# Norms fed from inside the matmul pairs, four modulation blocks moved to TensorE, matmuls without use in the gaps, and a result stored in four parts

## The chip, the cores and the metric

The kernel runs on one core of one Trainium2 chip. The metric is the device time of one execution in microseconds (us). Three executions of the kernel before are shown, and one more that was profiled.

## What is computed

Two layers of a decoder trunk at width 1024, 256 positions, batch 1, all in float32. What matters here is the frame around the mixers:

```python
for l in range(DEPTH):                       # 2 layers
    mod = (c_act @ w_mod[l] + b_mod[l])[:, None, :]       # 1024 x 6144 matrix times one vector
    sh1, sc1, gt1, sh2, sc2, gt2 = jnp.split(mod, 6, axis=-1)
    h = rmsnorm(x, norm1_g[l]) * (1 + sc1) + sh1
    z = h @ w_cat                            # then three mixers: RG-LRU, attention, RWKV-7
    ...
    x = x + gt1 * (merged @ w_out[l])
    h2 = rmsnorm(x, norm2_g[l]) * (1 + sc2) + sh2
    x = x + gt2 * conv_gated_mlp(h2, ffn_up[l], ffn_conv_w[l], ffn_conv_b[l], ffn_down[l])
return rmsnorm(x, final_g)
```

So there are five norms: before and after the mixers of each layer, and one at the end. Each needs a sum of squares over all 1024 channels, and nothing behind it can start before that sum.

## The kernel before

The residual stream X and the normed input H lie in SBUF as 8 tiles of 128 channels by 256 positions. The weights come in "pairs" of 1 MB, 75 for each layer, through a ring of four slots that the SyncE queue (SP) fills; the slot of pair g may be refilled when pair g - 4 is done. A pair makes two output tiles (m = 0 and 1) in one PSUM bank, g % 4. Pairs 35 to 38 of a layer (`OU`) are the output projection, 39 to 62 (`UP`) the up projection, 63 to 74 (`DN`) the down projection. In these three each factor is split into a high and a low part: ScalarE copies the high half (`out_high`, `high`, lines L642 and L666), VectorE subtracts the low one (`out_low`, `low`, L1157 and L1196), and TensorE runs three passes (`passes`, L1305 to L1307) of 8 matmuls for each tile, 48 for a pair. The other pairs are plain float32 matmuls (L1318, L1428); the profile shows two records for each of those.

Every engine has its own instruction list, written out in a fixed order, with counting semaphores between them. Around the change the order is this:

- ScalarE in the output projection: `out_high(0)`, `out_high(1)`, the high parts of the merged input, `out_high(2)`, `out_high(3)`, `high(0, 0, True)`, `high(0, 1, True)` (the first two pairs of the up projection), and only then `squares(2 * l + 1)`. `out_high(3)` waits for the second pair of the projection to be done, since it overwrites its weights; `high(0, 1, True)` waits for its ring slot, which is refilled after that same pair.
- ScalarE in the down projection: `high` of the last pair, whose second half waits for the end of the pair two before it, then `squares` of the next norm.
- VectorE: `residual(g, j, scale)` adds the two tiles of pair j to X (L1184), between the `low` calls; then `norm` makes H (L840) and, for the second norm of a layer, the low part `HL` (L1209).
- TensorE: after the last pair of a projection `ones_sum(n)` sums the 8 squared tiles with a matrix of ones (L1289), 8 matmuls that each wait for their square.

`squares(n)` squares X tile by tile, waits for the sum, takes Ln (L451), then Exp with scale -0.5 (L453) for the inverse root. `shifts` adds the modulation vector (L464, L465).

The modulation vectors are made beside all that. Each of the 12 vectors (`unit` u) is a sum over 8 blocks of 128 x 1024: VectorE multiplies a block with a scalar per partition and adds it to `macc` (L803 for the first block of a unit, L806 for the others), and `mod_sum` on TensorE (L1283) sums `macc` over the partitions with 8 matmuls of one column. Units 0 and 1 are needed for the first norm; their 16 blocks come in 8 transfers of 1 MB at the beginning. The others come through `mring`, two slots filled from GpSimd's queue, and `mod_beside(n)` puts n blocks between other work of VectorE. 16 of these blocks lie in the down projection of layer 0 (`DN_BLOCKS`), and the last `mod_sum(7)` comes after its last pair.

## Time and profile before

| what | us |
| --- | --- |
| median of three executions | 1295.5 |
| lowest and highest of them | 1282.28 and 1296.42 |
| the profiled execution, its whole time | 1285.15 |
| its span from the first to the last instruction | 1283.3 |
| TensorE busy in the span | 1197.8 (93%) |
| VectorE busy | 716.7 (56%) |
| ScalarE busy | 451.7 (35%) |

The span is what the trace covers; 1.85 us of the profiled execution lie around it. In the trace PE is a matmul on TensorE, PEld a weight load, DVE VectorE, ACT ScalarE, POOL GpSimd, and a q behind a name its queue. "PEclk" is the granted clock of TensorE as a share of 2.4 GHz: 1.00 is 2.4 GHz and 0.50 is 1.2 GHz.

### The profile page before, as it was taken

How to read it: one execution, taken by the hardware profiler on the slowest of the kernel's cores; microseconds unless marked ns; L12 is line 12 of the kernel's file. 1: busy time of each engine (PE TensorE's matmuls, PEld its weight loads, DVE VectorE, ACT ScalarE, POOL GpSimd, SP SyncE). 2: the span in 40 equal slices, each digit the busy share in tenths (PEclk: the TensorE clock that was granted, in tenths of full speed). 3: DMA queues.
4: the chain of work that ended last, by engine and by line, in shares of the span. 5: the costliest groups of instructions: out<-in, count | busy, mean ns of one | idle time of the engine just before them, and what ended most of it. 6: DMA issues, size and time to landing. Idle time of an engine off the chain costs nothing.

```text
span 1283.3 us, 23717 instructions
## 1 busy us (share of the span) xinstructions
PE 1197.8 (93%) x9976; PEld 1088.6 (85%) x9976; DVE 716.7 (56%) x1112; ACT 451.7 (35%) x747; POOL 65.8 (5%) x108
## 2 busy tenths in 40 slices
PE   2899999998999799999989999999899979999996
PEld 2788888877788799999968788888787879999996
DVE  5565545365236578777536482625522556778643
ACT  2222234401113666654232221450012156666532
POOL 0000000011010000001100000000100200000000
PEclk8799999999999899999989999999889999999998
DMA  9655444154135355557835454234512453454530
GB/s 381 258 206 187 165 141 178 45 208 154 66 127 183 152 195 177 182 187 290 294 113 188 174 188 166 106 132 155 169 56 84 147 215 121 175 196 166 194 132 33
DMA packets 38897, 214.57 MB, mean 167 GB/s; under 512 B 6144, under 2 KB 6400, under 8 KB 19232
## 3 DMA queue, kind: packets, MB, share of 16 engines
q1 hardware_dynamic: 27296, 171.42, 36.9%
q0 software_dynamic: 11520, 41.95, 9.5%
q8 instruction: 65, 1.06, 0.3%
q14 instruction: 16, 0.13, 0.0%
HBM read 212.30 MB, written 1.05 MB: 166 GB/s over the span
## 4 chain that ended last, share of the span: by engine, by line
PE 86%; DMA 5%; DVE 5%; issue 1%; ACT 1%; SPq 0%; DVEq 0%; ACTq 0%
PE ps L1318 19%; PE ps L1428 12%; PE ps L1305 12%; PE ps L1306 11%; PE ps L1307 11%; PE ps L1629 6%; DMA mring<-wmod_dram 4%; DVE macc L806 3%; PE ps L1514 3%; PE ps L1283 2%; PE ps L1289 1%; DMA G<-wmod_dram 1%; DVE H L840 1%; PE ps L1505 1%; PE ps L1439 1%
## 5 line engine op out<-in xcount | busy, mean ns | idle before, releaser
L1318 PE MATMUL ps<-H,ring 128*128 128x256 f32 x1088 | 244.4, 386 | 5.0 <-ACT H L465 5.0
L1318 PEld LDWEIGHTS ps<-H,ring 128*128 128x128 f32 x1088 | 210.0, 194 | 41.4 <-issue 12.6
L1196 DVE TENSOR_TENSOR WLO<-ring,WH 128x1024 fp32r<-128x1024 f32 x144 | 175.1, 1222 | 101.2 <-ACT WH L666 101.0
L1305 PE MATMUL ps<-HH,WH 128*128 128x256 f32 x768 | 219.5, 286 | 12.5 <-DVE HL L1209 12.5
L1306 PE MATMUL ps<-HL,WH 128*128 128x256 f32 x768 | 219.2, 285 | 0.0
L1307 PE MATMUL ps<-HH,WLO 128*128 128x256 f32 x768 | 219.1, 285 | 0.0
L666 ACT ACTIVATE WH<-ring 128x1024 fp32r<-128x1024 f32 x144 | 151.8, 1058 | 170.8 <-PE ps L1307 168.7
L1428 PE MATMUL ps<-H,ring 128*128 128x256 f32 x768 | 182.6, 390 | 0.0
L1428 PEld LDWEIGHTS ps<-H,ring 128*128 128x128 f32 x768 | 144.1, 193 | 22.7 <-issue 1.8
L1305 PEld LDWEIGHTS ps<-HH,WH 128*128 128x128 f32 x768 | 149.4, 195 | 13.3 <-issue 13.3
L1306 PEld LDWEIGHTS ps<-HL,WH 128*128 128x128 f32 x768 | 149.4, 195 | 0.0
L1307 PEld LDWEIGHTS ps<-HH,WLO 128*128 128x128 f32 x768 | 149.3, 194 | 0.0
L806 DVE SCALAR_TENSOR_TENSOR macc<-mring,sm,macc 128x1024 f32<-128x1024 f32 x70 | 89.8, 1283 | 46.2 <-DMA mring<-wmod_dram 43.2
L1305 PE MATMUL ps<-GH,WH 128*128 128x256 f32 (+1 forms) x384 | 108.7, 283 | 0.0
L1306 PE MATMUL ps<-GL,WH 128*128 128x256 f32 (+1 forms) x384 | 108.7, 283 | 0.0
L1307 PE MATMUL ps<-GH,WLO 128*128 128x256 f32 (+1 forms) x384 | 108.7, 283 | 0.0
L400 POOL DMA_DIRECT2D mring<-wmod_dram x80 | 42.5, 532 | 796.3 <-DVE macc L803 403.4
L563 ACT ACTIVATE G<-ps 128x512 f32<-128x512 f32 x24 | 14.1, 594 | 190.3 <-PE ps L1428 190.1
L1224 DVE SCALAR_TENSOR_TENSOR TK<-ps,PR,TK 128x255 f32<-128x255 f32 x192 | 79.1, 474 | 0.1
L1514 PEld LDWEIGHTS ps<-R 64*64 64x64 f32 x1792 | 57.2, 140 | 20.9 <-DVE R L1082 14.9
L1306 PEld LDWEIGHTS ps<-GL,WH 128*128 128x128 f32 x384 | 73.7, 192 | 0.0
L1307 PEld LDWEIGHTS ps<-GH,WLO 128*128 128x128 f32 x384 | 73.7, 192 | 0.0
(297 smaller groups left out, 1537.2 us busy)
## 6 DMA issues: line engine op xcount, KB each, us to landing
ring<-wmain_dram SPq DMA_DIRECT2D x150, 1024.0 KB, 4.8
mring<-wmod_dram POOLq DMA_DIRECT2D x80, 512.0 KB, 4.9
G<-wmod_dram SPq DMA_DIRECT2D x3, 1024.0 KB, 9.7
R<-wmod_dram SPq DMA_DIRECT2D x3, 1024.0 KB, 18.1
TK<-wmod_dram SPq DMA_DIRECT2D x2, 1024.0 KB, 23.1
C<-consts_dram SPq DMA_DIRECT2D x1, 1088.5 KB, 18.2
X<-x_t_dram SPq DMA_DIRECT2D x1, 1024.0 KB, 12.0
SW<-small_dram SPq DMA_DIRECT2D x2, 512.0 KB, 15.0
```

What stands on the lines that cost most here:

```text
L400: pool.dma_start(mring[:, n % 2, :], wmod[n]).then_inc(s_m[n % 2], 16)
L666: A(WH[:, n % 2, part], ring[:, b, part], ACT.Copy).then_inc(hi_ready, 1)
L806: V.scalar_tensor_tensor(macc[:, :], block, sm[:, CSIL + kt:CSIL + kt + 1], macc[:, :], ALU.mult, ALU.add).then_inc(mod_used, 1)
L1196: V.tensor_tensor(WLO[:, n % 2, part], ring[:, b, part], WH[:, n % 2, part].bitcast(F32), ALU.subtract).then_inc(lo_ready, 1)
L1224: ins = V.scalar_tensor_tensor(UB[:, q % 2, t, d:S], duo(b)[:, t, 0:S - d], PR[:, l, bass.ds(j + (COL["fw"] + 48 * (2 - d)), 1)], UB[:, q ...
L1305: MM(out, w_high[:, at], high, start=start, stop=False, skip_group_check=True)
L1306: MM(out, w_high[:, at], low, start=False, stop=False, skip_group_check=True)
L1307: return MM(out, w_low[:, at], high, start=False, stop=stop, skip_group_check=True)
L1318: last = MM(ps[:, g % 4, m * S:(m + 1) * S], w_of(g, m, i), rhs[:, i, :], start=(i == 0), stop=(i == KT - 1))
L1428: last = MM(ps[:, g % 4, m * S:(m + 1) * S], w_of(g, m, i), H[:, i, :], start=(i == 0), stop=(i == KT - 1))
L1514: last = MM(ps[halves[c], b, m * 64:(m + 1) * 64], a[halves[c], m, :], bb[halves[c], m, :], start=True, stop=True)
L1629: last = MM(ps[:, b, (m % 2) * S:(m % 2 + 1) * S], w_of(g, m, k, 4), y[:, k, :], start=(k == 0), stop=(k == 3))
```

## The change

1. **Beginning.** `macc` has two buffers, one for even and one for odd units. Four of the first 16 blocks (3, 7, 11, 15, `DIRECT`) no longer go through VectorE; `mod_direct` multiplies them on TensorE straight into the bank of their unit, 8 matmuls of one column each. GpSimd waits for the last of the first transfers before it loads `mring`. The first weight pair is issued ahead of the constants. The first four tiles of H may be made before unit 1 is known. 18 matmuls without use (`keep_clock`) lie between the parts.
2. **Norms.** `squares` and `ones_sum` no longer wait for the whole projection. After pair 1 of the last four TensorE sums tiles 0 and 1, after pair 2 tiles 2 and 3, between the two halves of pair 3 tiles 4 and 5, then 6 and 7. Tile 7 gets a bank of its own (`residual_ps`), so that tile 6 can be read while tile 7 is summed. ScalarE loads the table of Ln ahead of the squares, and `Acol` is made ahead of the residuals.
3. **Second norm of a layer.** HL is made by VectorE from the unshifted H, so ScalarE writes only HH. The first up pair (`up_first`) does its passes with HH first and those with HL after them.
4. **Gaps.** `keep_clock(8)` after three of the sums of squares in the two layers.
5. **Modulation in layer 0.** 10 of the 16 blocks move from the down projection into the up projection (`UP_BLOCKS`), whose VectorE loop is unrolled; the other 6 go one to each of the first six down pairs. `mod_sum(6)` comes after down pair 1 and `mod_sum(7)` after down pair 6.
6. **Output.** Four transfers of 256 KB, each when its two tiles are ready, in place of one of 1 MB.

```diff
+DIRECT = (3, 7, 11, 15)
+UP_BLOCKS = [0] * 4 + [1, 0] * 10
+DN_BLOCKS = [1, 1, 1, 1, 1, 1, 0, 0, 0, 0, 0, 0]
+DN_SUM, DN_LAST = 1, 6
+LOGARITHM = "natural_log"
...
+        def residual_ps(g, j, i):
+
+            return ps[:, 5, 0:S] if (j, i) == (3, 1) else ps[:, g % 4, i * S:(i + 1) * S]
...
+            sp.dma_start(ring[:, 0, :], wmain[0]).then_inc(s_w[0], 16)
             sp.dma_start(C[:, :], consts).then_inc(s_par, 16)
...
-            sp.wait_ge(h_pre, 8 * 5)
-            sp.dma_start(y_t, H[:, :, :]).then_inc(s_out, 16)
-            sp.wait_ge(s_out, 16)
+            for j in range(4):
+                sp.wait_ge(h_pre, 8 * 4 + 2 * j + 2)
+                sp.dma_start(y_t[:, 2 * j:2 * j + 2, :], H[:, 2 * j:2 * j + 2, :]).then_inc(s_out, 16)
+            sp.wait_ge(s_out, 64)
...
+            pool.wait_ge(s_first[7], 16)
...
             def squares(n):
 
+                if n:
+                    act.preload_act_table_set(LOGARITHM)
+                else:
+                    act.wait_ge(s_x, 16)
                 for m in range(KT):
-                    if n:
+                    if n and m % 2 == 0:
+                        act.wait_ge(x_tile, 4 * (n - 1) + m // 2 + 1)
+                    elif n:
                         g = PAIRS * ((n - 1) // 2) + (OU if n % 2 else PAIRS - 4) + m // 2
                         act.wait_ge(bank_free[g % 4], EMPTIED[g][g % 4] + 1)
-                    if m == 0 and n:
-                        act.wait_ge(pair_done, PAIRS * ((n - 1) // 2) + (OU + 4 if n % 2 else PAIRS))
-                    elif m == 0:
-                        act.wait_ge(s_x, 16)
                     A(H[:, m, :], X[:, m, :], ACT.Square).then_inc(x_sq, 1)
...
-                    V.tensor_tensor(HL[:, m, :], H[:, m, :], HH[:, m, :].bitcast(F32), ALU.subtract).then_inc(hl_ready, 1)
+                    V.scalar_tensor_tensor(HL[:, m, :], H[:, m, :], mod[:, u, m:m + 1], HH[:, m, :].bitcast(F32),
+                                           ALU.add, ALU.subtract).then_inc(hl_ready, 1)
...
+            def mod_direct(n):
+
+                u, kt = divmod(n, 8)
+                pe.wait_ge(s_first[n // 2], 16)
+                for j in range(KT):
+                    MM(ps[:, 7 - u, j:j + 1], first_blocks(n // 2)[:, n % 2, j * P:(j + 1) * P], sm[:, CSIL + kt:CSIL + kt + 1],
+                       start=(n % 8 == DIRECT[0] and j == 0), stop=False, skip_group_check=True)
...
+            def keep_clock(n, b, moving):
+
+                for _ in range(n):
+                    MM(ps[:, b, 0:S], ones[:, :], moving, start=True, stop=True, skip_group_check=True)
...
+                    pe.wait_ge(c_ready, 1)
+                    mod_direct(3)
+                    ones_sum(0)
+                    keep_clock(6, 5, X[:, 0, :])
+                    mod_direct(7)
+                    keep_clock(2, 5, X[:, 0, :])
                     mod_sum(0)
+                    keep_clock(4, 5, X[:, 0, :])
+                    mod_direct(11)
+                    keep_clock(6, 5, X[:, 0, :])
+                    mod_direct(15)
                     mod_sum(1)
...
+                        if (j, m) == (3, 0):
+                            last.then_inc(out_half, 1)
+                            ones_sum(2 * l + 1, 4, 6)
                     last.then_inc(pair_done, 1)
-                ones_sum(2 * l + 1)
+                    if j:
+                        ones_sum(2 * l + 1, (0, 2, 6)[j - 1], (2, 4, 8)[j - 1])
+                keep_clock(8, 6, C[:, 0:S])
...
+                for q in range(4):
+                    down(2, q, tail=True)
+                    if q:
+                        ones_sum(2 * l + 2, (0, 2, 6)[q - 1], (2, 4, 8)[q - 1])
+                if l == 0:
+                    keep_clock(8, 6, C[:, 0:S])
```

## Rows read from the trace of the kernel before

**Rows 1.** The page: busy time and share of two engines.

```profile
PE 1197.8 (93%) x9976; PEld 1088.6 (85%) x9976; DVE 716.7 (56%) x1112; ACT 451.7 (35%) x747; POOL 65.8 (5%) x108
```

**Rows 2.** Timeline of the beginning: start, duration, engine, line, what, idle before.

```profile
6.71 0.75 DVE L803 TENSOR_SCALAR macc<-G,sm 128x1024 f32<-128x1024 f32 x1 [2.19 <-DMA G<-wmod_dram]
...
11.43 2.67 DVE L806 SCALAR_TENSOR_TENSOR macc<-G,sm,macc 128x1024 f32<-128x1024 f32 x2 [2.57 <-DMA G<-wmod_dram]
...
30.51 5.45 DVE L806 SCALAR_TENSOR_TENSOR macc<-TK,sm,macc 128x1024 f32<-128x1024 f32 x4
...
36.01 3.57 PE L1283 MATMUL ps<-sm,macc 128*128 128x1 f32 x16 [10.65 <-DVE macc L806]
...
41.07 30.70 PE L1318 MATMUL ps<-H,ring 128*128 128x256 f32 x128 [1.48 <-ACT H L465]
```

**Rows 3.** The last first-block transfers (tile TK): issue range, and time to landing.

```profile
L342 SPq DMA_DIRECT2D TK<-wmod_dram x2: 482/4467/8452, 5.0 to 5.5; - x2
...
DMA to landing us min/median/max: 22.1/23.1/24.1
```

**Rows 4.** The chain of work: start, duration, what; plain matmuls and `mod_sum` at 2.4 GHz.

```profile
97.30 1.68 PE ps L1283 x16
...
132.05 13.81 PE ps L1318 x64
```

**Rows 5.** ScalarE's timeline around the second norm of layer 0.

```profile
408.79 1.92 ACT L642 ACTIVATE OWH<-ring 128x2048 fp32r<-128x2048 f32 x1 [3.84 <-PE ps L1307]
410.61 1.99 ACT L666 ACTIVATE WH<-ring 128x1024 fp32r<-128x1024 f32 x2
413.66 2.01 ACT L666 ACTIVATE WH<-ring 128x1024 fp32r<-128x1024 f32 x2 [1.06 <-DMA ring<-wmain_dram]
420.58 2.56 ACT L449 ACTIVATE H<-X 128x256 f32<-128x256 f32 x8 [4.92 <-PE ps L1307]
...
425.30 1.28 ACT L453 ACT_TABLE_LOAD   x1
426.60 0.42 ACT L453 ACTIVATE RT<-RT 128x256 f32<-128x256 f32 x1
...
439.11 1.06 ACT L666 ACTIVATE WH<-ring 128x1024 fp32r<-128x1024 f32 x1 [1.75 <-PE ps L1307]
```

**Rows 6.** VectorE's timeline around the same norm.

```profile
407.25 0.87 DVE L1184 SCALAR_TENSOR_TENSOR X<-ps,sm,X 128x256 f32<-128x256 f32 x2
...
427.11 3.26 DVE L840 SCALAR_TENSOR_TENSOR H<-X,Acol,RT 128x256 f32<-128x256 f32 x8 [5.92 <-ACT RT L453]
```

**Rows 7.** The chain of work there: split passes before and after, and the sum of squares.

```profile
419.97 0.12 PE ps L1306
...
421.05 3.73 PE ps L1289 x16
...
430.85 0.55 PE ps L1305
```

**Rows 8.** Windows: us, busy PE, PEld, DVE, ACT, POOL, granted clock, DMA share, GB/s.

```profile
26.00:36.00 10.00, 0.00 (x0) 0.00 (x0) 9.23 (x8) 0.00 (x0) 0.00 (x0) 0.50 1.03 416
...
428.00:430.00 2.00, 0.00 (x0) 0.00 (x0) 2.00 (x6) 2.00 (x6) 0.00 (x0) 0.77 0.61 258
```

**Rows 9.** Between the layers: ScalarE's last weight half; then the chain of work.

```profile
630.95 1.06 ACT L666 ACTIVATE WH<-ring 128x1024 fp32r<-128x1024 f32 x1 [1.76 <-PE ps L1307]
...
655.79 4.60 PE ps L1318 x10
```

**Rows 10.** VectorE in the up projection of layer 0: its only idle time in a tile.

```profile
457.48 1.23 DVE L1196 TENSOR_TENSOR WLO<-ring,WH 128x1024 fp32r<-128x1024 f32 x1 [1.17 <-ACT WH L666]
```

**Rows 11.** The end: when ScalarE takes the last weights, last norm, store.

```profile
1257.78 1.06 ACT L666 ACTIVATE WH<-ring 128x1024 fp32r<-128x1024 f32 x1 [1.76 <-PE ps L1307]
...
1275.82 3.25 DVE L840 SCALAR_TENSOR_TENSOR H<-X,PR,RT 128x256 f32<-128x256 f32 x8 [5.64 <-ACT RT L453]
...
y_dram<-H SPq DMA_DIRECT2D x1, 1024.0 KB, 3.9
```

More of the change, by code:

```diff
@@ L100, with added @@
 EMPTIED = _emptied()
+def added(n):
+    return n + 1 - sum(d <= n for d in DIRECT)
 FILL = [4, 16, 24, 16, 16, 4, 12, 8] + [8] + [3, 5, 4] * 4 + [6, 6, 0]
@@ L1248, in _ @@
                     up_tile(0, q, True)
-                with dve.Fori(1, FT // 4) as i:
-                    for q in range(4):
-                        up_tile(i, q)
+                if l == 0:
+                    for n in range(4, FT):
+                        up_tile(n // 4, n % 4)
+                        mod_beside(UP_BLOCKS[n])
+                else:
+                    with dve.Fori(1, FT // 4) as i:
+                        for q in range(4):
+                            up_tile(i, q)
                 hidden_low(0, FT - 2)
@@ L1672, in up @@
                         for k in range(KT):
-                            if first and q == 0 and m == 0:
-                                pe.wait_ge(hl_ready, KT * l + k + 1)
                             last = passes(ps[:, b, m * S:(m + 1) * S], WH[:, q % 2, :], WLO[:, q % 2, :], m * KT + k, HH[:, k, :], HL[:, k, :], k == 0, k == KT - 1)
                         last.then_inc((half_done, pair_done)[m], 1)
-                for q in range(4):
-                    up(0, q, True)
+                up_first()
+                for q in range(1, 4):
+                    up(0, q)
                 with pe.Fori(1, FT // 4) as i:
@@ L1682, in _, with down @@
                         up(i, q)
-                def down(i, q, first=False):
+                def down(i, q, first=False, tail=False):
                     g = PAIRS * l + DN + q
@@ L1695, in down @@
                             at = k if first else bass.ds(i * 8 + k, 1)
[L1696 to L1697 removed]
+                            last = passes(residual_ps(g, q, m), WH[:, q % 2, :], WLO[:, q % 2, :], m * KT + k, GH[:, at, :], GL[:, at, :],
+                                          first and k == 0 and (m == 0 or q == 3), False)
                         last.then_inc((half_done, pair_done)[m], 1)
+                        if (tail, q, m) == (True, 3, 0):
+                            ones_sum(2 * l + 2, 4, 6)
                 for q in range(4):
                     down(0, q, True)
+                    if l == 0 and q == DN_SUM:
+                        mod_sum(6)
+                pe.wait_ge(g_ready, FT * (l + 1))
                 if l == 0:
[L1703 to L1712 removed]
+                    for q in range(4):
+                        down(1, q)
+                        if 4 + q == DN_LAST:
+                            mod_sum(7)
+                else:
+                    with pe.Fori(1, 2) as i:
                         for q in range(4):
                             down(i, q)
[L1715 removed]
+                for q in range(4):
+                    down(2, q, tail=True)
+                    if q:
+                        ones_sum(2 * l + 2, (0, 2, 6)[q - 1], (2, 4, 8)[q - 1])
+                if l == 0:
+                    keep_clock(8, 6, C[:, 0:S])
 def kernel(x, c, positions, w_mod, b_mod, norm1_g, norm2_g, final_g, w_in, w_merge_a, w_merge_b, w_merge_c, w_out,
```

135 lines of the change are left out of this document (74 added, 61 removed).

## The prediction

> **What bounds the kernel now.** I read the page first. TensorE is busy for 93% of the span and VectorE for 56% [rows 1], so time can come only from places where TensorE waits or runs slowly. The timeline then shows where those are. The one long wait is at the beginning: TensorE's product starts at 41.07 us, behind a modulation sum at 36.01 that waited 10.65 us for VectorE's blocks [rows 2]. The others are the four later norms. At the one in layer 0 the split passes end at 420.1 and the next begins at 430.85; between them lie 3.73 us of sums of squares [rows 7] and ScalarE's chain of Ln, a table load and Exp [rows 5]. The windows show a second cost of each gap: the granted clock is 0.50 (1.2 GHz) while TensorE is nearly idle at the beginning, and falls within 428 to 430, in the gap behind the sum of squares [rows 7, 8]. Then work restarts slowly: the first 10 records of layer 1 take 4.60 us [rows 9], 0.46 each, against 13.81 / 64 = 0.216 at the full 2.4 GHz [rows 4].
>
> Unit prices at full clock: a plain matmul is two records, 0.432 us; a split pass 0.12 [rows 7], so a pair of 48 is 5.76; a `mod_sum` 1.68 [rows 4], and a `mod_direct` issues the same 8 one-column matmuls, so I take 1.68 for it too.
>
> **Beginning (part 1).** The last two first-block transfers are issued at 5.0 and 5.5 and land 22.1 and 24.1 us later [rows 3], at 27.1 and 29.6. Block group 1 landed 4.72 us after group 0 (6.71 and 11.43, [rows 2]), where 2.56 separate others (27.1 to 29.6): the 1 MB of `mring` went in between. Holding it back moves the last group to about 27.05. VectorE then has 12 blocks for 16, at 5.45 / 4 = 1.36 each [rows 2], and is no longer last: block 14 ends at about 28.5. What is last is either the landing or TensorE's own list. By the landing: 27.05 + 1.68 + 1.68, then the vector, ScalarE's shift and the start, together 41.07 - 39.6 = 1.5 less what is made ahead (0.8), gives a start at 31.3. By the list: it opens with group 1 (8.9) and holds 4 directs and 2 sums (10.1 us), 8 matmuls of squares (3.5) and 18 without use (7.8), 21.4 us at full clock, and some 4.5 us of it run at half speed first (2.3 lost): the sum ends at 32.6, and the start is 33.4. The list is later and I take it: 41.07 - 33.4 = 7.7. If the clock is also kept, the four first pairs take 27.6 (128 x 0.216) in place of 30.70 [rows 2], 3.1 more. Together **-10.8**. The bounds: 9.8 + 3.1 = -12.9 by the landing alone, and nearly nothing (-2) if the useless matmuls don't bring the clock up, since each of the list's parts then takes double. The added wait of GpSimd holds only `mring` loads that nobody needs for 15 us; the weight pair now ahead of the constants delays `derived`, which has the first pair's 7 us as cover.
>
> **Second norm of a layer (parts 2 to 4).** This is where I expect a wait in the place of the one removed. TensorE now stops after pair 1 of the output projection for squares 0 and 1. ScalarE reaches its squares only behind `out_high(3)`, `high(0, 0)` and `high(0, 1)`, and the first of these itself starts when that pair ends: 408.79, then 410.61, then 413.66 (after a transfer that is issued at the same moment), done at 415.67 [rows 5]. Behind it comes the table load that the change puts ahead of the squares, 1.28 [rows 5], and one square, 2.56 / 8 = 0.32 pitch and 0.42 long: TensorE goes on at about 417.5, idle for **8.7 us**. VectorE is not to blame, its first residual ends at 408.1 [rows 6]. Before, the same engine time of ScalarE lay beside pairs 2 and 3. In the shorter gap from 424.8 to 430.85 the granted clock fell from 1.00 to 0.50 [rows 7, 8], so this one costs the clock as well: 2.3 (half of 4.6, [rows 9]).
>
> From there: second square and sum to 418.4; pair 2 with the clock loss 5.76 + 2.3, to 426.4; sums of tiles 2 and 3, 0.86; half of pair 3, 2.88; sums of 4 and 5, 0.86; second half to 433.9. Behind it only tile 7: residual 0.48 [rows 6], square 0.42, one sum 0.43 and the handovers, 1.4, to 435.3. Ln, load and Exp take what they take now (424.78 to 427.02, 2.24 [rows 5, 7]), to 437.55. H, HH and the start: 1.2, to 438.75. `up_first` follows ScalarE's pace of 0.4 for 8 tiles, 3.1, then 16 + 16 + 8 and some passes, in all 6.85: the first up pair ends at 445.6. Before it ended at 439.05 (ScalarE's wait for it ends at 439.11 [rows 5]). So this norm **loses 6.6** in each layer, although its tail behind the last pass shrinks (420.1 to 430.85 was 10.7; 433.9 to 438.75 is 4.9). Both: **+13.2**, with layer 1 taken as equal. `keep_clock(8)` is 3.46, inside the 3.45 from 435.3 to the start, so it costs nothing and keeps the up projection at full clock.
>
> The load ahead of the squares sits in this stall, but without it it would sit behind them. The row prices it at 1.28 and lets the next activation begin 1.30 after its start (425.30, 426.60 [rows 5]). The Trainium skill, ScalarE: Activation LUTs, section "What ACT_TABLE_LOAD costs", gives about 2.66 for every switch to a different set, with a drain behind the load. The trace does not agree (1.30); by the page each stall would be 1.4 longer, +5.5 in the four norms.
>
> **Between the layers (parts 2, 4, 5).** ScalarE's last weight half starts when the second of the last four pairs has ended, 630.87 [rows 9]; `mod_sum(7)` now lies ahead of that, so 632.55. From this point, called E: weight half and table load to E + 2.4; VectorE's low half and first residual to E + 2.8; squares; TensorE idle until E + 3.3, sums to E + 4.2. Then 5.76 + 0.86 + 2.88 + 0.86 + 2.88 to E + 17.4; tile 7 and its sum to E + 18.85; Ln, load, Exp to E + 21.1; H, shift and start 1.25: E + 22.35 = 654.9. Before, the product started at 655.79 [rows 9]: 0.9 won. With the clock kept another 2.9, as at the beginning (4.60 - 10 x 0.216 = 2.4, and a little behind it). **-3.8**. What is removed here is VectorE's late last block and the sum of all eight squares behind the last pass; what comes is the 3.3 stall.
>
> **Up projection (part 5).** Ten blocks of 1.28 or less join VectorE, one in two tiles. A tile has 1.17 idle there [rows 10], two have 2.3, so the block fits; the low weight halves are wanted some 5 us later than they are made. Zero. If that cover is gone, 10 x 1.28 = 12.8. `mring` adds 0.5 MB per 11.5 us beside 2 MB.
>
> **End (parts 2, 6).** E is 1257.75 [rows 11]. Exp ends at E + 21.1 = 1278.85, against 1275.79: the stall of 3.3 and six sums (2.6) ahead of the last pass, less 2.8 behind it. Eight tiles of H take 3.25 [rows 11], to 1282.15. The store took 3.9 from issue [rows 11]; a quarter of it is bounded by 1.0 and 3.9, and since 1 MB at the 416 GB/s of the first window [rows 8] is 2.5, I take 3.9 - 1.9 = 2.0. End 1284.4, **+1.1**.
>
> **The clock in the 3.3 us stalls.** The gap at 424.8 that cost the clock was longer, 6 us [rows 7, 8]; whether one of 3.3 costs it, no row shows. I count one fall in two, **+2.3**; ends 0 and +4.6.
>
> **Sum.** -10.8 + 13.2 - 3.8 + 1.1 + 2.3 = +2.0 on the profiled execution's 1285.15: 1287.2. That execution and the lowest of the three stand some 10 us under the other two (1295.5, 1296.42), and the median is one of the upper. On the median the same sum gives 1297.5. I can't tell from one trace which level the next median takes, and put the forecast in the middle, 1292. 2% (25.9 us) is about what a measurement of this kernel can tell from no change.
>
> **Rivals.**
> - *Squares are not late* (0.05). ScalarE's order would have to let them ahead of the weight copies. The order in the code and the copy at 413.66 [rows 5] speak against it. Then each second norm is 8.7 + 2.3 earlier, 4.4 won in place of 6.6 lost; the two later stalls (3.3 each) and the clock go too: -10.8 - 8.8 - 7.1 - 2.2 = -28.9, or 1256.
> - *The clock is not kept* (0.13). The useless matmuls are few, and one-column matmuls may not hold the clock: at 36.01 they ran at 3.57, half speed [rows 2]. Then the beginning wins 5 rather than 10.8, the layer change 0.9, the first up pairs lose 2.2 each, both short stalls cost: 2.0 + 5.8 + 2.9 + 4.4 + 2.3 = +17.4, or 1302.6 to 1313.
> - *VectorE becomes late in the up projection* (0.05): slower than before. Mechanism: blocks wait for their transfer, the low weight halves behind them on VectorE come late, and TensorE waits for those. The point from which it decides is a delay over 5 us, one pair's worth. Price 12.8 and up to 3 us for each of three late transfers: +24, or 1309 to 1320.
> - *Ln and Exp in one table* (0.03). The row shows a load ahead of each [rows 5]. If the named set held both, one load less on the path of four norms, -5.1: 1282 to 1292. The Trainium skill, ScalarE: Activation LUTs, section "Table sets: the hidden batching unit", says that one set holds both and that Ln then Exp needs one load; the trace before has two, and the set named in the change is the one of Ln.
> - *The change does what I say* (0.74).
>
> **Range and chances.** From the main case: the beginning's own bounds are 2 us down and 9 up, the clock 2.3 either way, on levels of 1287 and 1297: 1280 to 1306. It should reach into the clock case and some way to the early-squares case: 1272 to 1308. Faster by over 2%: only the early squares, 0.05. Slower by over 2%: the upper end of the VectorE case and of the clock case, 0.04. Same 0.91.
>
> **What the next profile would show.** Product start near 33 with a granted clock of 1.00; TensorE's sum of squares after output pair 1 waiting over 8 us for ScalarE, in both layers, and a granted clock of 0.50 behind it; waits near 3.3 in the last down pairs; the product of layer 1 at full clock; VectorE in the up projection with no idle time in every second tile and TensorE without gaps. I am wrong if that first wait is short, if the beginning starts before 31 or after 38, or if passes in the up projection wait for low halves.

## The result, and the profile after

| kernel | median us | lowest to highest | executions |
| --- | --- | --- | --- |
| before | 1286.45 | 1279.33 to 1296.42 | 20 |
| changed | 1294.01 | 1289.33 to 1304.71 | 20 |

The change makes the kernel slower: ratio 1.0072, 95% interval 1.005 to 1.0094, that is +9.3 us (+6.4 to +12.1) on 1286.45. The profiled execution took 1296.32, its span is 1294.5. The ratio and its interval are those of the record and not the quotient of the two medians, which differ by 7.6 us. Of the three executions that were known at the time of the forecast two lay high; with 20 of them the median of before is 9 us lower. That the forecast of 1292 is near 1294 is luck: its level was too high, its sum of +2.0 too small, and the two errors met. Against the 1295.5 that was known, 1292 stood for a small gain, and the kernel got slower. One execution of all that are used here, 1290.91 of late_sums_out_only, was in a slower state of the chip; its kernel's ratio leaves it out.

**Where the 11.2 us between the two spans lie.** I cut both spans at the starts of the four groups of 128 plain records in the chain of waits: the products at the head of each layer's mixers, and the plain pairs at their end. The lines show start and duration. Of the changed kernel:

```profile
39.16 29.86 PE ps L1366 x128
...
364.87 27.75 PE ps L1686 x128
...
661.71 27.86 PE ps L1366 x128
...
997.72 27.75 PE ps L1686 x128
```

Of the kernel before:

```profile
41.07 30.70 PE ps L1318 x128
...
367.24 27.75 PE ps L1629 x128
...
655.79 30.53 PE ps L1318 x128
...
996.19 27.75 PE ps L1629 x128
```

| stage | before | changed | difference |
| --- | --- | --- | --- |
| 1: start to product, layer 0 | 41.07 | 39.16 | -1.9 |
| 2: product to end of the mixers, layer 0 | 326.2 | 325.7 | -0.5 |
| 3: output projection, MLP, up to product of layer 1 | 288.5 | 296.8 | +8.3 |
| 4: mixers, layer 1 | 340.4 | 336.0 | -4.4 |
| 5: output projection, MLP, last norm, store | 287.1 | 296.8 | +9.7 |

This table is the instrument for all that follows. In the kernels below stage 3 repeats within 0.7 us and stage 5 within 1.3 where their code is the same, while stages 2 and 4, whose code nobody touches, range over 12 and 10 us. So I read norms and the end from stages 3 and 5 of a single trace; what lies in stages 2 and 4 only a median over many executions averages out. Stage 1 doesn't repeat: seven traces have the beginning of the change, and their product starts at 36.02, 36.12, 36.92, 36.96, 37.18, 39.16 (the one above) and 43.73. One start can't be told from another by less than some 3 us; the rows inside the beginning say more.

**The second norm of layer 0.** ScalarE's timeline (start, duration, engine, line, what, idle before), to be laid beside [rows 5]:

```profile
406.41 1.91 ACT L662 ACTIVATE OWH<-ring 128x2048 fp32r<-128x2048 f32 x1 [3.84 <-PE ps L1355]
408.23 1.99 ACT L686 ACTIVATE WH<-ring 128x1024 fp32r<-128x1024 f32 x2
411.66 2.00 ACT L686 ACTIVATE WH<-ring 128x1024 fp32r<-128x1024 f32 x2 [1.45 <-DMA ring<-wmain_dram]
413.68 1.28 ACT L459 ACT_TABLE_LOAD   x1
414.98 1.33 ACT L468 ACTIVATE H<-X 128x256 f32<-128x256 f32 x4
```

The weight copies stand ahead of the squares as they did, but now TensorE waits for the first square. TensorE's own timeline and the chain of waits, against [rows 7]:

```profile
415.45 2.08 PE L1331 MATMUL ps<-H,ones 128*128 128x256 f32 x4 [9.13 <-ACT H L468]
```

```profile
406.35 5.29 DMA ring<-wmain_dram
...
432.31 0.70 PE ps L1331 x2
433.01 3.45 PE ps L1338 x16
...
436.53 5.13 PE ps L1738 x32
```

A stall of 9.1 us: 5.3 until the weights for ScalarE's last two copies have landed, 2.0 for these copies, 1.3 for the table load, 0.4 for the square. Then a short tail: the last sum ends at 433.0, useless matmuls fill until `up_first`. The first up pair ends at 443.58, 37.25 after output pair 1 (406.33); before it was 439.05 - 408.72 = 30.33. So 6.9 us are lost here. In layer 1 the stall is 8.54 us, and between the same two points lie 37.8 us in place of 30.0, so 7.8 are lost. The windows (us, busy PE, PEld, DVE, ACT, POOL, granted clock, DMA share, GB/s) show the clock, to be compared with [rows 8]:

```profile
406.00:408.00 2.00, 0.32 (x3) 0.11 (x1) 0.00 (x0) 1.59 (x1) 0.00 (x0) 1.00 0.40 86
408.00:410.00 2.00, 0.00 (x0) 0.00 (x0) 1.65 (x1) 2.00 (x3) 0.00 (x0) 0.61 0.85 348
...
418.00:420.00 2.00, 2.00 (x16) 2.00 (x16) 0.00 (x0) 0.00 (x0) 0.00 (x0) 0.83 0.03 8
```

It falls to 0.50 (1.2 GHz) in the stall and comes back within 418 to 420.

**Between the layers and at the end.** The two stalls of the down projection: 3.33 us ahead of 640.51, where the clock fell (0.63 in 640 to 642, 0.52 in the next two), and 3.25 us at the end, where it didn't. Here it is VectorE's residual and then ScalarE's square that TensorE waits for, by the chain of the end:

```profile
1269.32 0.49 DVE X L1209
1269.83 0.43 ACT H L468
1270.30 1.13 PE ps L1331 x4
```

The four stores, issued at 1289.6 to 1292.0, land 2.2 us after their issue, the one of before 3.9 [rows 11].

**The beginning.** TensorE's timeline, against [rows 2]:

```profile
11.55 3.54 PE L1315 MATMUL ps<-sm,G 128*128 128x1 f32 x16 [11.55 <-DMA G<-wmod_dram]
14.96 5.84 PE L1331 MATMUL ps<-H,ones 128*128 128x256 f32 x16
20.63 2.75 PE L1338 MATMUL ps<-X,ones 128*128 128x256 f32 x12
23.22 1.84 PE L1315 MATMUL ps<-sm,R 128*128 128x1 f32 x16
...
33.76 1.84 PE L1315 MATMUL ps<-sm,TK 128*128 128x1 f32 x16
35.47 2.74 PE L1324 MATMUL ps<-sm,macc 128*128 128x1 f32 x16
```

TensorE is never idle from 11.55 to 38.21, so its own list sets the start, as foreseen, but the list is 26.7 us long and not 23.7. Its first parts run at half pace (3.4 and 5.7 us from start to start, where a `mod_direct` later takes 1.7 and 8 wide matmuls 3.46), and its last sum is slow again (2.74 for 1.84). And the clock is not kept for the product, by the windows:

```profile
34.00:36.00 2.00, 2.00 (x20) 2.00 (x20) 0.00 (x0) 0.00 (x0) 0.00 (x0) 1.00 1.03 420
36.00:38.00 2.00, 2.00 (x13) 2.00 (x12) 0.00 (x0) 0.00 (x0) 0.00 (x0) 0.59 0.99 404
38.00:40.00 2.00, 1.05 (x3) 0.90 (x4) 1.76 (x7) 1.50 (x4) 0.00 (x0) 0.50 1.02 420
```

### The profile page after: what moved, and what is told of

Its sections match the earlier page's. It is cut to its first block, busy times and chain, and to the rows that moved or that the text cites. A ratio compares the mean times of both kernels' runs of the same rounds, so it can differ in the third digit from the quotient of the medians.

```text
span 1294.5 us, 23732 instructions
## 1 busy us (share of the span) xinstructions
PE 1218.7 (94%) x10124; PEld 1105.5 (85%) x10124; DVE 712.4 (55%) x1108; ACT 446.9 (35%) x731; POOL 66.0 (5%) x108
## 4 chain that ended last, share of the span: by engine, by line
PE 88%; DMA 5%; DVE 3%; ACT 2%; issue 1%; SPq 0%; DVEq 0%; POOL 0%; ACTq 0%; POOLq 0%
PE ps L1366 18%; PE ps L1353 12%; PE ps L1355 12%; PE ps L1354 12%; PE ps L1485 11%; PE ps L1686 6%; DMA mring<-wmod_dram 4%; PE ps L1571 2%; PE ps L1331 2%; PE ps L1324 2%; DVE macc L826 1%; PE ps L1338 1%; PE ps L1738 1%; DMA ring<-wmain_dram 1%; DMA G<-wmod_dram 1%
## 5 line engine op out<-in xcount | busy, mean ns | idle before, releaser
L1353 PE MATMUL ps<-HH,WH 128*128 128x256 f32 x736 | 208.3, 283 | 0.0
L1354 PE MATMUL ps<-HL,WH 128*128 128x256 f32 x736 | 208.3, 283 | 0.0
L1355 PE MATMUL ps<-HH,WLO 128*128 128x256 f32 x736 | 208.3, 283 | 0.0
L1353 PEld LDWEIGHTS ps<-HH,WH 128*128 128x128 f32 x736 | 141.3, 192 | 0.0
L1354 PEld LDWEIGHTS ps<-HL,WH 128*128 128x128 f32 x736 | 141.3, 192 | 0.0
L1355 PEld LDWEIGHTS ps<-HH,WLO 128*128 128x128 f32 x736 | 141.3, 192 | 0.0
L1353 PE MATMUL ps<-GH,WH 128*128 128x256 f32 x384 | 110.5, 288 | 0.0
L1354 PE MATMUL ps<-GL,WH 128*128 128x256 f32 x384 | 108.9, 284 | 0.0
L1355 PE MATMUL ps<-GH,WLO 128*128 128x256 f32 x384 | 108.9, 284 | 0.0
L826 DVE SCALAR_TENSOR_TENSOR macc<-mring,sm,macc 128x1024 f32<-128x1024 f32 x70 | 89.8, 1282 | 33.4 <-DMA mring<-wmod_dram 30.7
L1571 PEld LDWEIGHTS ps<-R 64*64 64x64 f32 x1792 | 56.5, 139 | 21.0 <-DVE R L1102 14.7
L1353 PEld LDWEIGHTS ps<-GH,WH 128*128 128x128 f32 x384 | 74.1, 193 | 0.2
```

The source lines that it names most:

```text
L826: V.scalar_tensor_tensor(macc[:, u % 2, :], block, sm[:, CSIL + kt:CSIL + kt + 1], macc[:, u % 2, :], ALU.mult, ALU.add).then_inc(mod_used, 1)
L1353: MM(out, w_high[:, at], high, start=start, stop=False, skip_group_check=True)
L1354: MM(out, w_high[:, at], low, start=False, stop=False, skip_group_check=True)
L1355: return MM(out, w_low[:, at], high, start=False, stop=stop, skip_group_check=True)
L1571: last = MM(ps[halves[c], b, m * 64:(m + 1) * 64], a[halves[c], m, :], bb[halves[c], m, :], start=True, stop=True)
```

## The experiments

Twelve kernels, each compared with executions of the kernel before on its own chip, whose medians there are 1284.0 to 1285.4. The median is taken over 5 to 12 executions; the three columns on the right come from one trace each. The ratio is that of the record; the quotient of the medians differs from it by up to 0.0015, which is 2 us. Differences between two of the kernels below are often differences between chips as well. "Stages 3 + 5" is 575.7 before and 593.6 for the changed kernel.

| kernel | median us | ratio to before, 95% | product starts | stage 2 | stages 3 + 5 |
| --- | --- | --- | --- | --- | --- |
| late_sums | 1267.91 | 0.9872 (0.9841 to 0.9903) | 43.73 | 324.7 | 563.3 |
| no_start_fill | 1294.06 | 1.0074 (1.005 to 1.0097) | 35.80 | 334.2 | 595.2 |
| no_gap_fill | 1302.16 | 1.0149 (1.0114 to 1.0184) | 37.18 | 323.3 | 597.3 |
| late_sums_no_start_fill | 1266.86 | 0.9854 (0.9822 to 0.9886) | 34.96 | 335.0 | 563.4 |
| begin_only | 1280.87 | 0.9954 (0.9926 to 0.9983) | 36.92 | 328.0 | 575.9 |
| late_sums_out_only | 1278.13 | 0.9957 (0.9928 to 0.9987) | 36.12 | 323.5 | 572.6 |
| early_squares | 1279.28 | 0.9943 (0.9914 to 0.9971) | 36.02 | 328.6 | 571.2 |
| joint_table | 1262.69 | 0.9838 (0.9802 to 0.9873) | 36.96 | 326.6 | 560.0 |
| old_begin | 1296.96 | 1.0107 (1.0066 to 1.0147) | 37.12 | 326.2 | 594.9 |
| fill_after | 1262.97 | 0.982 (0.9782 to 0.9857) | 47.70 | 322.7 | 560.0 |
| lean_start | 1261.32 | 0.9829 (0.9795 to 0.9863) | 34.86 | 326.6 | 559.4 |
| short_fill | 1259.27 | 0.979 (0.9766 to 0.9814) | 37.82 | 331.0 | 558.7 |

**late_sums: all of the first six sums between the halves of the last pair.** The same matmuls in another place; nothing between the pairs waits for ScalarE any more.

```diff
                         if (j, m) == (3, 0):
                             last.then_inc(out_half, 1)
-                            ones_sum(2 * l + 1, 4, 6)
+                            ones_sum(2 * l + 1, 0, 6)
...
-                    if j:
-                        ones_sum(2 * l + 1, (0, 2, 6)[j - 1], (2, 4, 8)[j - 1])
+                    if j == 3:
+                        ones_sum(2 * l + 1, 6, 8)
```

and the same two edits in the down projection.

> The changed kernel with one edit: the sums of squares 0 to 5 lie together between the two halves of the last pair of each projection, none behind the second or third of the last four pairs. Theory 1 (ScalarE's order: TensorE waits for squares that come behind weight copies): the wait of 9.1 us in each second norm and its clock loss of 2.1 go, the waits of 3.3 in the down projections and one clock loss of 2 go; in all -30 us against the changed kernel, a ratio of 0.982 to before. Theory 2 (it is the sums and the split last pair themselves, wherever they stand): within 5 us of the changed kernel.

Measured 1267.91, 26 us below the changed kernel, where 30 were expected, and 16 (12 to 20) below the kernel before. Stages 3 + 5 fall by 30.3. ScalarE still does its squares behind the weight copies, but they are done as TensorE comes to them; its and TensorE's timelines:

```profile
416.91 1.28 ACT L459 ACT_TABLE_LOAD   x1
418.21 1.95 ACT L468 ACTIVATE H<-X 128x256 f32<-128x256 f32 x6
```

```profile
418.68 2.86 PE L1331 MATMUL ps<-H,ones 128*128 128x256 f32 x12
...
425.95 3.62 PE L1338 MATMUL ps<-C,ones 128*128 128x256 f32 x16
429.63 0.36 PE L1738 MATMUL ps<-HH,WH 128*128 128x256 f32 x1
```

TensorE's idle time at this norm is 0.6 us. So the place of the first sums is what makes the change slower, and the rest of it is worth some 16 us.

**late_sums_out_only: the same in the output projections alone.** Only the first of the two pairs of edits.

> The changed kernel with late sums in the two output projections, the down projections left as changed. Theory 1: the two waits of 9.1 us with their clock loss go, -21 us against the changed kernel, a ratio of 0.990; the waits of 3.3 us in the down projections stay. Theory 2 (half of the gain of the late sums came from the down projections): -13 us, 0.997.

Measured 1278.13, 16 below the changed kernel, where 21 were expected (15 by the two ratios); stages 3 + 5 fall by 21.0. So 5 us of what the two stages gain don't arrive in the median, and in early_squares, below, 8. Both profiled executions are the fastest of their kernels (1271.82 and 1269.42); where the rest goes in the others no trace shows. The difference to late_sums, 9.2 in stages 3 + 5, is what the sums between the down pairs cost. Their two stalls are 3.33 and 3.25 us here as well. The granted clock stays at 1.00 in all windows around the first, and falls behind the second (0.82, 0.50 and 0.82 in 1244 to 1250), so a part of the 2.6 beyond the stalls is that fall.

**early_squares: only ScalarE's order.** The sums stay where the change puts them; the squares go between the weight copies.

```diff
                 out_high(2)
+                squares(2 * l + 1, 0, 2)
                 out_high(3)
...
                 high(0, 0, True)
+                squares(2 * l + 1, 2, 4)
                 high(0, 1, True)
-                squares(2 * l + 1)
+                squares(2 * l + 1, 4)
```

> The changed kernel with all sums where the change put them, and only ScalarE's order changed in the output projection: squares 0 and 1 before the fourth weight copy, 2 and 3 behind the first half-pair copy of the up projection. Theory 1 (the wait is for ScalarE's order, not for the place of the sums): the waits of 9.1 us go here too, -21 us against the changed kernel, 0.990, the same as late sums in the output projections. Theory 2 (sums behind pair 1 are bad in themselves, a transfer or a residual is also late): the wait only shrinks to 3 to 5 us, -10 us.

Measured 1279.28, 15 below the changed kernel (17 by the two ratios), where one theory said 21 and the other 10. Stages 3 + 5 fall by 22.5, and TensorE no longer waits for the first square; of the idle time at this norm 0.6 is left, at the last one. ScalarE's timeline, and then TensorE's at the first square:

```profile
402.29 1.28 ACT L459 ACT_TABLE_LOAD   x1
405.02 0.81 ACT L468 ACTIVATE H<-X 128x256 f32<-128x256 f32 x2 [1.45 <-DVE X L1213]
406.11 1.91 ACT L664 ACTIVATE OWH<-ring 128x2048 fp32r<-128x2048 f32 x1 [0.27 <-PE ps L1359]
```

```profile
405.85 1.02 PE L1335 MATMUL ps<-H,ones 128*128 128x256 f32 x4
```

It and late_sums_out_only are two unlike cures for one stall, and both win nearly the same. That settles the cause: ScalarE's squares stand behind its weight copies and the transfer for which the last of them wait. It is not VectorE and not the act of summing in between. The table load, 1.28 of the 9.13 us, moved together with the squares, so its part was not separated.

**no_gap_fill: without the useless matmuls behind the sums.** The calls in their three places go.

```diff
-                keep_clock(8, 6, C[:, 0:S])
...
-                if l == 0:
-                    keep_clock(8, 6, C[:, 0:S])
```

> The changed kernel without the three groups of eight matmuls without use behind the norms' sums. Theory 1 (they keep the granted clock at 1.00 through ScalarE's Ln and Exp): the first up pair of each layer and the first product of layer 1 run at 0.50 for some 4 us, +2 to +3 us each, +7 in all. Theory 2 (a gap of 3.5 us alone doesn't cost the clock here): 0.

Measured 1302.16, 8 slower than the changed kernel; stages 3 + 5 grow by 3.7 and the product of layer 1 takes 29.55 in place of 27.86, 1.7 more. That is 5.4 in the trace, 8 on the medians. The windows:

```profile
432.00:434.00 2.00, 0.74 (x4) 0.73 (x5) 1.91 (x5) 1.39 (x4) 0.00 (x0) 0.92 1.00 418
434.00:436.00 2.00, 2.00 (x11) 2.00 (x10) 2.00 (x6) 1.92 (x5) 0.00 (x0) 0.50 1.02 430
```

Without them the clock falls as the first up pair begins; with them it is 1.00 in all windows from 434 to 442. These matmuls do what they are for.

**no_start_fill: without those in the beginning.** **late_sums_no_start_fill** is the same on late_sums.

```diff
-                    keep_clock(6, 5, X[:, 0, :])
                     mod_direct(7)
-                    keep_clock(2, 5, X[:, 0, :])
                     mod_sum(0)
-                    keep_clock(4, 5, X[:, 0, :])
                     mod_direct(11)
-                    keep_clock(6, 5, X[:, 0, :])
                     mod_direct(15)
```

> The changed kernel without the 18 matmuls without use in the beginning. Theory 1 (TensorE's own list is last there, and the one-column matmuls at its end lose the clock anyway): the product of layer 0 starts 3 to 5 us earlier than 39.2, at half clock as before; -4 us. Theory 2 (the transfers are last, and the matmuls keep the clock for most of the list): the start stays or comes later, since the one-column matmuls run at half speed, 0 to +4 us.

> Both edits, late sums and no matmuls without use in the beginning. If the two are independent, -34 us against the changed kernel: a ratio near 0.979 to before.

Measured 1294.06 and 1266.86: no difference to the kernels with them (1294.01 and 1267.91). TensorE's list is 25 us and its end at half pace:

```profile
31.30 3.55 PE L1324 MATMUL ps<-sm,macc 128*128 128x1 f32 x16
```

In both kernels the granted clock falls within 22 to 24 (0.51 and 0.53), earlier than in any trace with these matmuls, and yet the product starts earlier too (35.80 and 34.96), since 18 matmuls less have to run. In both traces stage 2 is some 9 us longer than elsewhere, with a mean granted clock of 0.97 where the others have 0.98 to 1.00. These executions were the slowest of their kernels (1297.49 of 8, 1270.29 of 6), so it may be chance. But -4 us and more were expected and nothing came; whether an earlier start is lost again in stage 2 these runs don't settle.

**begin_only: the kernel before with the new beginning and nothing else**: the two accumulators, `DIRECT`, GpSimd's wait, the first weight pair ahead, four tiles of H ahead and the useless matmuls there. The core of it, on the kernel before:

```diff
+DIRECT = (3, 7, 11, 15)
...
-        macc = sb("macc", [P, D])
+        macc = sb("macc", [P, 2, D])
...
+            pool.wait_ge(s_first[7], 16)
...
-            mod_unit(0)
-            mod_unit(1)
+            for n in range(FIRST):
+                if n not in DIRECT:
+                    mod_block(n)
+            mod_vector(0)
```

> The kernel before with the new beginning alone (two accumulators, four blocks on TensorE, its matmuls without use, the first weight pair ahead of the constants). Theory 1 (TensorE's list of 26.7 us takes the place of VectorE's blocks and the clock falls all the same): -1 to -4 us, a ratio of 0.997 to 0.999. Theory 2 (the beginning is worth what was forecast): -10.8 us, 0.992.

Measured -5.9 us by the ratio (-9.5 to -2.2), -4.6 by the medians, between the two expectations and clear of -10.8. The start is 4.15 earlier, and the product takes 29.65 in place of 30.70, so about 1 us more is won. TensorE's list runs from 9.33 to 35.97:

```profile
9.33 3.54 PE L1290 MATMUL ps<-sm,G 128*128 128x1 f32 x16 [9.33 <-DMA G<-wmod_dram]
12.73 5.63 PE L1306 MATMUL ps<-H,ones 128*128 128x256 f32 x16
...
33.03 2.94 PE L1299 MATMUL ps<-sm,macc 128*128 128x1 f32 x16
```

26.6 us again. What differs from the trace after is only when group 1 had landed, 9.2 against 11.4.

**old_begin: the changed kernel without the new beginning.** Only the two accumulators, the first weight pair and the four tiles of H ahead stay.

```diff
-DIRECT = (3, 7, 11, 15)
+DIRECT = ()
...
-            pool.wait_ge(s_first[7], 16)
...
-                    mod_direct(3)
                     ones_sum(0)
-                    keep_clock(6, 5, X[:, 0, :])
-                    mod_direct(7)
-                    keep_clock(2, 5, X[:, 0, :])
                     mod_sum(0)
-                    keep_clock(4, 5, X[:, 0, :])
-                    mod_direct(11)
-                    keep_clock(6, 5, X[:, 0, :])
-                    mod_direct(15)
                     mod_sum(1)
```

> The changed kernel with the beginning of the kernel before: no blocks on TensorE, no matmuls without use in the beginning, GpSimd loads as before; everything else as changed. If the terms add up (the beginning alone gave -5.9 us, the change as a whole +7 to +9), this stands at +13 to +15 us over the kernel before, ratio about 1.011, with the product at about 41 us. If the beginning's gain is lost again in the mixers whenever the norms are changed as well (a rival that the kernel without the filling matmuls suggested: its product started 3.4 us earlier and the mixers lost 9), it stands at +7 to +9, ratio 1.006, no slower than the changed kernel.

Measured 1.0107, +13.7 us (8.5 to 18.9), as expected; 13.7 - 5.9 = 7.8 against 9.3. But this is a weak proof that the terms add up, because the product starts at 37.12 and not at 41: this kernel already has most of what the new beginning moves. In the kernel before, VectorE stood still in the middle of its blocks, until `mod_sum(0)` had freed the one `macc`; its timeline:

```profile
19.58 2.67 DVE L806 SCALAR_TENSOR_TENSOR macc<-R,sm,macc 128x1024 f32<-128x1024 f32 x2
25.40 0.17 DVE L812 TENSOR_TENSOR mod<-ps,PR 128x8 f32<-128x8 f32 x1 [3.15 <-PE ps L1283]
```

With two buffers it goes on, and all 16 blocks are done at 32.5 instead of 36.0:

```profile
22.00 0.75 DVE L822 TENSOR_SCALAR macc<-R,sm 128x1024 f32<-128x1024 f32 x1
...
27.09 5.45 DVE L825 SCALAR_TENSOR_TENSOR macc<-TK,sm,macc 128x1024 f32<-128x1024 f32 x4
```

So in this trace the start is 4.0 us earlier, 3.4 of it by the second buffer and the rest by the tiles of H ahead, and the whole new beginning moved it as much in begin_only. The four blocks on TensorE, the held `mring` and the useless matmuls together bring the start no further forward in these traces: VectorE's blocks end at 28.57 in begin_only, but TensorE's list only at 35.97, about where the last sum of old_begin ends (36.16). What they save VectorE they put into TensorE's list. Whether they are worth something in another way (the medians differ by 3, the intervals overlap) stays open.

**joint_table: late_sums, with one table for Ln and Exp.**

```diff
-LOGARITHM = "natural_log"
+LOGARITHM = "natural_log_exp_and_others"
```

> Late sums in all projections, and ScalarE loads the set that holds Ln and Exp together ahead of the squares, in place of the one of Ln. Theory 1: the load between Ln and Exp goes in four norms, -1.28 us each, -5.1 against late sums (0.9872), a ratio of 0.983. Theory 2: a load before Exp stays, 0.

Measured 1262.69 against 1267.91. The load between Ln and Exp is gone:

```profile
421.92 0.47 ACT L470 ACTIVATE RT<-ps,sm 128x256 f32<-128x256 f32 x1 [0.79 <-PE ps L1331]
422.42 0.42 ACT L472 ACTIVATE RT<-RT 128x256 f32<-128x256 f32 x1
```

From Ln to the next weight copy ScalarE needs 8.38 us (421.92 to 430.30) in place of 9.65 in late_sums, so this norm's tail wins 1.27. But stages 3 + 5 together fall by 3.3, not by 4 x 1.28 = 5.1: stage 5, with two norms, by 2.7, and stage 3 by 0.7. In stage 3 TensorE waits 0.81 us for the first square (ahead of 414.43), which it didn't in the trace of late_sums, and the second of its norms keeps almost nothing: ahead of layer 1 the useless matmuls, 3.45 us, now outlast what they covered. TensorE goes without a pause from them to the product, whose first tile of H was begun at 642.18:

```profile
640.44 3.62 PE L1338 MATMUL ps<-C,ones 128*128 128x256 f32 x16
643.89 11.39 PE L1366 MATMUL ps<-H,ring 128*128 128x256 f32 x52
```

**fill_after: on joint_table, the last six useless matmuls of the beginning moved behind the last block, four more behind the last sum.**

```diff
-                    keep_clock(6, 5, X[:, 0, :])
                     mod_direct(15)
+                    keep_clock(6, 5, X[:, 0, :])
                     mod_sum(1)
+                    keep_clock(4, 5, X[:, 0, :])
```

> The kernel with late sums and the joint table, with the last six useless matmuls of the beginning moved behind the last block on TensorE, and four more behind the last modulation sum. Theory A: the granted clock falls at the end of the list because the last 32 one-column matmul records don't hold it, so with wide matmuls between and behind them the product of layer 0 starts at full clock: its 128 records take 27.9 us rather than 29.7, and the start is at 37.0 as before; 2 us off 1262.7, about 1260.7. Theory B: the fall has nothing to do with what runs there (it came at about 34 to 36 us in three kernels whatever stood there), then 29.7 again and 1262.7.

Measured 1262.97, no difference. In the profiled execution (the slowest of six, 1271.74; the fastest took 1257.39) the clock fell at about 27, by the windows, and most of the rest of the list ran at half speed, useless matmuls too, until the product started at 47.70.

```profile
26.00:28.00 2.00, 2.00 (x17) 1.98 (x16) 1.86 (x2) 0.00 (x0) 0.00 (x0) 0.81 1.07 442
```

The product then ran at full clock, 27.63, 2 won for 11 lost. The fall came ahead of the edit, as in late_sums (24 to 26), in a window in which TensorE was busy for all of its 2.00 us. So the edit didn't cause it, and this trace tests neither theory as it was meant, with a fall at 34 to 36; that the clock was back for the product fits the first.

**lean_start: on joint_table, without the ten useless matmuls ahead of the last two blocks.**

```diff
-                    keep_clock(4, 5, X[:, 0, :])
                     mod_direct(11)
-                    keep_clock(6, 5, X[:, 0, :])
                     mod_direct(15)
```

> The kernel with late sums and the joint table, without the ten useless matmuls that stand ahead of the last two blocks on TensorE. TensorE's own list is what ends last in the beginning, 26.7 us long; these ten are 4.5 of it. The last block lands at about 27.5 and VectorE ends at 28.5 to 31, so the last sum ends at about 33 and the product starts at 34 rather than 37. If the list sets the start, 3 us earlier; by the clock falling a bit earlier, half of it is lost (x128 at 30): 1260.5 to 1262.5. Rival: the clock falls much earlier, as without any of these matmuls, and the start comes no sooner than 35 at half clock: 1262.7 or more.

Measured 1261.32, in the expected range; the difference of 1.4 to joint_table is inside the intervals. The start is at 34.86, between the 34 of the forecast and the 35 of the rival. The clock fell within 26 to 28 here, and the shorter list still ended 2.1 earlier. But short_fill, below, has the same beginning, its clock fell within 24 to 26, and its product starts at 37.82: a fall 2 us earlier cost 3 us.

**short_fill: on lean_start, five useless matmuls behind each sum of squares in place of eight.**

```diff
-                keep_clock(8, 6, C[:, 0:S])
+                keep_clock(5, 6, C[:, 0:S])
```

at both places.

> The kernel with late sums, the joint table and the lean beginning, with five useless matmuls behind each sum of squares in place of eight. With the table load gone, the eight (3.46 us) are longer than what they cover: the product of layer 1 starts 3.45 us after they begin though its first tile of H is ready about 1 us before. Five last 2.16. If the clock is still kept: stage from the output of the mixers of layer 0 to the product of layer 1 279.8 to 278.5, the last stage 0.3 shorter, in all 1.3 to 1.6 us, median about 1260, ratio 0.982. If five are too few to keep the clock: the product of layer 1 takes over 29 us rather than 27.63 and the first up pairs 2 us more each, and the kernel is no faster than 1261.3, perhaps 1266.

Measured 1259.27, ratio 0.979 (0.9766 to 0.9814): 27 us below the kernel before and 35 below the changed one, the lowest median of all. Stages 3 + 5 are 558.7 against 559.4, stage 3 0.9 less and stage 5 0.2 more, where 1.6 in all were expected; the clock is kept:

```profile
645.37 2.32 PE L1338 MATMUL ps<-C,ones 128*128 128x256 f32 x10
647.76 7.58 PE L1366 MATMUL ps<-H,ring 128*128 128x256 f32 x34
```

The product starts 2.39 after the first of them, where it was 3.45, and takes 27.86 for 27.63. The step against lean_start is too small for the medians to show.

## Why the prediction was wrong

The sum said +2.0 and the kernel is +9.3 (+6.4 to +12.1). The stall and its cause were foreseen rightly; the gain of the beginning, which should have paid for most of it, was sized at nearly double of what it is. Term by term, forecast and then the profiled execution:

- **Beginning, -10.8: this is the step that failed.** Measured -1.9 for the start and -0.8 for the product's pace, -2.7; over many executions, by begin_only, -5.9 (-9.5 to -2.2). In the trace it holds 8.1 of the 9.2 us between the sum and the spans. Two parts of it were wrong. First, "the sum ends at 32.6": TensorE's list was rightly taken as what is last, but sized with only 2.3 us at half speed. The rows of begin_only show (3.4 - 1.7) + (5.5 - 3.5) = 3.7 at its head and 2.94 - 1.7 = 1.2 at its tail, 4.9 in all where 2.3 were counted; with a beginning at 9.3 for 8.9 and 0.3 in the rest it ends at 36.0. In the trace after it ends 2.2 later again because group 1 landed at 11.4. No trace with this list comes near the forecast start of 33.4; the earliest is 36.02. Second, "the clock is also kept", -3.1: in all seven traces of this beginning the product begins at half clock and takes 29.55 to 30.66, not 27.6, and only 0.8 of the term came. What I didn't see is that VectorE's 3.15 us wait for the one `macc` was the cheap thing to remove: it stands in the timeline of before between 22.25 and 25.40. By old_begin the second buffer gives 3.4 of its 4 us without a single block on TensorE.
The rival "the clock is not kept" priced the beginning at -5, near the -5.9 of begin_only; its parts on the gaps did not come (the up pairs and the product of layer 1 run at full clock).
- **Second norms, +13.2: right.** Stall forecast 8.7, measured 9.1 and 8.5; loss forecast 6.6 each, measured 6.9 and 7.8. early_squares shows the named cause: with ScalarE's order changed alone, stages 3 + 5 are 22.5 shorter. That this is more than 13.2 is no contradiction: the forecast was against the kernel before, the cure lets the shorter tail through (the same reckoning gave 4.4 won for 6.6 lost in the rival, 22.0 for both).
- **Between the layers, -3.8 and the one clock fall, +2.3: right together.** Of 0.9 won in time, measured 1.4 lost: the difference is the clock fall in the stall at 640.5, which was counted apart at 2.3. Of the two 3.3 us stalls one cost the clock, the other didn't. One fall in two was a guess that held here; over all six kernels that keep these stalls it was 9 of 12. The product of layer 1 takes 27.86 for 30.53, 2.7 of the 2.9.
- **Up projection, 0: right.** TensorE has no wait there. VectorE's ten blocks (8 of 1.28, 2 of 0.75 us) come out of its waits for ScalarE, which shrink from 26.0 to 16.8 us between 450 and 575.
- **End, +1.1:** measured 27.45 from E to the end for 25.55, +1.9. The store was sized right (2.2 us for a quarter against 2.0); the rest lies in the sums and the handovers.
- Stage 4 fell by 4.4, of which 2.7 is the product's; the rest is within what this stage varies by.

Together -2.7 + 14.7 - 1.3 + 1.9 = 12.6, with the remainders of stages 2 and 4 (+0.4 and -1.7) the 11.2 of the spans, to 0.1. The Trainium skill, ScalarE: Activation LUTs, section "What ACT_TABLE_LOAD costs", was weighed in the forecast and would have added 5.5 us. The trace after disagrees with it as the one before did: where nothing else is waited for, the activation again follows 1.30 after the start of the load (413.68, 414.98). The losses of 6.9 and 7.8 don't decide it: 1.4 more each on the forecast 6.6, an estimate from that figure, would be 8.0. The Trainium skill, ScalarE: Activation LUTs, section "Table sets: the hidden batching unit", names one set that holds both Ln and Exp; that rival fell for the change as it stands (the load at 433.54 is still there) and is confirmed by joint_table, 1.27 per norm where nothing else covers it.

The level also counts. I set the forecast between an execution of 1285 and a median of 1295.5 from three; the levels were not two but one spread of 17 us around 1286.

## What to carry to other kernels

When work of an engine is spread out so that it overlaps, look up what the other engine does at the new moment: a sum that comes earlier needs its input earlier, and here ScalarE's queue made that cost 9 us twice. Put the early parts as late as they still hide, or move the producer too. With the first alone the change goes from +9 to -16 us; with the second alone, in the output projections, to -7. Before moving work from a busy engine to one whose list is short, look for a wait in the middle of the busy engine's row: here a second buffer of 4 KB per partition, with four tiles of H made ahead, moved the start as far as all of the moved work did. And useless matmuls in a gap cost time once they outlast what they cover: when the covered chain got shorter, they held the product of layer 1 back by about 1 us.

## What the runs showed of the hardware that I had not expected

- At the start of the program TensorE runs at half pace although the granted clock in the rows is 1.00: from start to start its first 8 one-column matmuls take 3.4 us and later ones 1.7, the 8 wide ones behind them 5.1 to 6.6 us and later ones 3.46. The column can't be read as the pace there.
- The granted clock fell from 1.00 to 0.50 while TensorE was busy without a pause: within 32 to 34 in begin_only, 34 to 36 in joint_table, 36 to 38 after the change, within 26 to 28 in fill_after and lean_start. What stood in the list at that moment differed, and joint_table and late_sums, which have the same beginning, fell some 10 us apart. What decides it no run here settles. It sets the start: 43.73 in late_sums against 36.96 in joint_table, and 37.82 in short_fill against 34.86 in lean_start.
- A stall of 3.3 us sometimes costs the clock. It cost it in layer 0 of the changed kernel, but not at its end, nor in layer 0 of late_sums_out_only (3.33 us, clock 1.00 throughout). Over the six kernels that keep these stalls it fell in 9 of 12: five times of six in layer 0, four of six at the end. Stage 5 is 298.0 with the fall (no_start_fill, old_begin) and 296.8 without it (after the change).
- The landing of the first transfers varies by over 2 us from one execution to the next: TensorE's list, which waits for group 1 and starts the same way in all of them, begins between 9.11 (short_fill) and 11.55 (after the change).
- The mixers, with the same code, take 322.7 to 335.0 us in layer 0 and 330.5 to 340.4 in layer 1, with the clock falling in other places; a gain of 2 us elsewhere can't be read from one execution's total.
